# Values taken from a 384-column product and reordered over DRAM, in an attention phase on one core

## The reference

```python
hnorm = rms_norm(x, mixer_norm[layer])
qkv = (x @ w_in).reshape(b, s, 3, N_GROUPS, ATTN_HEADS, ATTN_HEAD_DIM)
for g, (window, dilation) in enumerate(((128, 1), (512, 4), (2048, 16))):
    q = rms_norm(qkv[:, :, 0, g], q_gain[g]) * (ATTN_HEAD_DIM ** -0.5)
    k = rms_norm(qkv[:, :, 1, g], k_gain[g])
    o, l = dilated_window_attention(q, k, qkv[:, :, 2, g], rel_bias[:, g], window, dilation)
wts = softmax(stack(lses), axis=0)
y = einsum('gbsh,gbshe->bshe', wts, stack(outs))
```

## Time and profile before

| | us |
|---|---|
| median of 3 runs (3330.32 to 3334.62) | 3331.82 |
| time of the profiled execution | 3333.34 |
| its span | 3331.6 |
| PE busy in it | 3162.4 (95%) |
| DVE, ACT, POOL busy | 1337.3, 1107.3, 824.0 |

### The profile page before, as it was taken

How to read it: one execution, slowest core, us unless ns; L and a number is a source line. 1 busy time by engine, 2 the same in 40 slices (tenths; PEclk the granted TensorE clock), 3 DMA queues, 4 the chain that set the end, 5 groups by cost and what they waited for, 6 DMA issues and landing times. The chain is left out here.

```text
span 3331.6 us, 48256 instructions
## 1 busy us (share of the span) xinstructions
PE 3162.4 (95%) x17466; PEld 2672.2 (80%) x17466; DVE 1337.3 (40%) x3725; ACT 1107.3 (33%) x3002; POOL 824.0 (25%) x598
## 2 busy tenths in 40 slices
PE   4999999999999995999999999899877999999999
PEld 3888888888888883878888888778665788888887
DVE  6446554555556554341313133531064431313131
ACT  4555555555555553321111112211254211111020
POOL 3333333333233310222222222222211222222221
PEclk9999999999999996999999999999898999999999
DMA  2112121221212114111111111111201111111112
GB/s 97 39 38 62 41 59 40 62 54 47 56 45 62 41 28 153 50 45 50 51 47 48 51 45 51 36 47 45 82 32 51 45 51 45 51 51 45 51 51 76
DMA packets 89904, 177.01 MB, mean 53 GB/s; under 512 B 25515, under 2 KB 55870, under 8 KB 89662
## 3 DMA queue, kind: packets, MB, share of 16 engines
q1 hardware_dynamic: 87358, 169.63, 16.4%
q10 hardware_dynamic: 2304, 4.20, 0.3%
HBM read 160.67 MB, written 13.12 MB: 52 GB/s over the span
## 5 line engine op out<-in xcount | busy, mean ns | idle before, releaser
L69 PE MATMUL ps_qk<-w_hi,attn_hT_hi 128*128 128x256 f32 x1536 | 439.1, 286 | 23.9 <-DVE attn_hT_lo L213 9.7
L915 POOL TENSOR_TENSOR first_w_lo<-first_raw,first_w_hi 128x1024 fp32r<-128x1024 f32 x96 | 231.5, 2411 | 886.0 <-ACT first_w_hi L911 886.0
L71 PE MATMUL ps_qk<-w_hi,attn_hT_lo 128*128 128x256 f32 x1536 | 437.6, 285 | 0.0
L70 PE MATMUL ps_qk<-w_lo,attn_hT_hi 128*128 128x256 f32 x1536 | 437.4, 285 | 0.0
L857 POOL TENSOR_TENSOR w_lo<-raw,w_hi 128x384 fp32r<-128x384 f32 x192 | 193.6, 1009 | 660.3 <-ACT w_hi L602 660.3
L915 POOL TENSOR_TENSOR second_w_lo<-second_raw,second_w_hi 128x1024 fp32r<-128x1024 f32 x72 | 172.3, 2393 | 620.6 <-ACT second_w_hi L911 620.6
L69 PEld LDWEIGHTS ps_qk<-w_hi,attn_hT_hi 128*128 128x128 f32 x1536 | 295.9, 193 | 28.2 <-issue 13.9
L70 PEld LDWEIGHTS ps_qk<-w_lo,attn_hT_hi 128*128 128x128 f32 x1536 | 296.6, 193 | 0.4
L71 PEld LDWEIGHTS ps_qk<-w_hi,attn_hT_lo 128*128 128x128 f32 x1536 | 296.4, 193 | 0.0
L69 PE MATMUL first_ps<-first_hid_hi,first_w_hi 128*128 128x512 f32 x640 | 250.9, 392 | 33.5 <-DVE first_hid_lo L1241 33.5
L635 ACT ACTIVATE prob<-ps_s,neg_max 128x128 f32<-128x128 f32 (+1 forms) x384 | 156.3, 412 | 362.4 <-DVE neg_max L726 362.4
(11 more groups left out here) (276 smaller groups left out, 6844.6 us busy)
## 6 DMA issues: line engine op xcount, KB each, us to landing
raw<-in_wqkv SPq DMA_DIRECT2D x192, 192.0 KB, 2.3
first_raw<-in_w SPq DMA_DIRECT2D x64, 512.0 KB, 3.4
second_raw<-in_w SPq DMA_DIRECT2D x64, 512.0 KB, 3.4
w_bc<-share_dram SPq DMA_DIRECT2D x48, 256.0 KB, 4.2
first_raw<-in_vo_pieces SPq DMA_DIRECT2D x16, 512.0 KB, 3.4
bias<-bias_dram SPq DMA_DIRECT2D x16, 256.0 KB, 3.4
yT_dram<-o_g SPq DMA_DIRECT2D x8, 512.0 KB, 3.1
first_raw<-in_attn_wo SPq DMA_DIRECT2D x8, 512.0 KB, 3.5
```

The source lines that it names most:

```text
L69: pe.matmul(out, a_hi, b_hi, start=first, stop=False)
L70: pe.matmul(out, a_hi, b_lo, start=False, stop=False)
L71: return pe.matmul(out, a_lo, b_hi, start=False, stop=last)
L915: pool.tensor_tensor(self.lo[:, n % 2, :], self.raw[:, n % self.RAW, :], self.hi[:, n % 2, :].bitcast(F32), ALU.subtract).then_inc(self.lo ...
```

## The change

What it does:

1. The value columns join the query and key columns: 24 products of 128x384 per step into `ps_qk` instead of 24 of 128x256 and 6 of 128x512. `ps_v`, `vT`, the transposes of `vT` and the two ACT copies per section are gone.
2. ACT copies the tile's values, 128x128, from `ps_qk` to `v_out` (a part of `ring`). SP writes them to `v_dram`, and after tiles 3 and 7 reads the half section back in the order of the group into `v_raw`.
3. ACT makes the high part of a unit's values out of `v_raw` (it was out of `ps_t`), and POOL the low part (DVE did it). On POOL it stands between the low part of the weights and `rs`.
4. PE's list is products, turned tiles, probabilities times values of the unit two back, turned probabilities of the unit one back, scores.
5. On ACT the turned tiles move from the end of the step to behind the exponentials, ahead of the outputs, the weights and the squares. On DVE they move from behind the sums of squares to behind the maxima.
6. The loop over supersteps is gone, all are written out.

```diff
-def run_supersteps(eng, step):
-    for st in range(LOOP_FIRST):
-        for j in range(TT):
-            step(0, st, j)
-    with eng.Fori(0, LOOP_COUNT) as i:
...
+def run_supersteps(step):
+    for st in range(LAST_SUPER + 1):
         for j in range(TT):
+            step(st, j)
...
+                if 1 <= T <= TT * SECTIONS:
+                    sec, t = divmod(T - 1, TT)
...
+                    sp.wait_ge(v_kept, T)
+                    sp.dma_start(v_dram[sec % 2, t * P:(t + 1) * P, :], v_out[:, t % 2, :]).then_inc(v_stored[t % 2], 16)
+                    if t % 4 == 3:
...
+                        for slot in range(2):
+                            sp.wait_ge(v_stored[slot], 16 * (T // 2))
+                        for dest, src in unit_order(sec, t // 4):
+                            sp.dma_start(dest, src).then_inc(v_in[t // 4], 16)
...
+                def products(ks):
...
+                    if T >= 2 and ks[0] == 0:
                         pe.wait_ge(qkn_done, T - 1)
-                    for k in range(KT):
+                        pe.wait_ge(v_kept, T - 1)
+                    for k in ks:
...
-                        mm = split_matmul(pe, ps_qk[j % 2][:, 0:2 * P],
+                        mm = split_matmul(pe, ps_qk[j % 2][:, 0:W3],
...
-                        mm = pe.transpose(ps_t[:, 2 * P:3 * P], vT[:, (st - 1) % 2, j * P:(j + 1) * P], ident[:])
...
-                    for k in range(2 * (j % 4), 2 * (j % 4) + 2):
-                        mm = split_matmul(pe, ps_v[:], w_hi[:, par, k, 2 * P:3 * P], w_lo[:, par, k, 2 * P:3 * P],
...
+                products(range(KT))
+                turn_tiles()
+                weigh_values()
+                turn_probabilities()
+                scores()
...
+                def unit_values():
+                    if has_unit(st, j, 1):
+                        sec, u = unit(st, j, 1)
+                        for half in halves_needed(sec, u):
+                            act.wait_ge(v_in[half], v_loads(sec))
+                        act.copy(v_hi[:, (U - 1) % 3, :], v_raw[:, sec % 2, u, :]).then_inc(v_hi_done, 1)
...
+                def squares_and_values():
...
+                        act.activation(sq[:], ps_qk[j % 2][:, 0:2 * P], ACT.Square).then_inc(squared, 1)
+                        if T >= 2:
+                            act.wait_ge(v_stored[j % 2], 16 * (T // 2))
+                        act.copy(v_out[:, j % 2, :], ps_qk[j % 2][:, 2 * P:W3]).then_inc(v_kept, 1)
...
+                exponentials()
+                turned_tiles()
+                outputs()
+                unit_values()
...
+                weights()
+                squares_and_values()
+                turned_probabilities()
...
+                        dve.wait_ge(rs_done, T + 1)
+                        dve.wait_ge(v_kept, T + 1)
...
+                maxima()
+                turned_tiles()
+                merge_step(st, j)
+                variances()
+                turned_probabilities()
+                normalise()
...
                     pool.wait_ge(w_hi_done, T + TT + 1)
                     lo_part(j % 4, (st + 1) % 2, j)
+                if has_unit(st, j, 1):
+                    sec, u = unit(st, j, 1)
+                    slot = (U - 1) % 3
+                    pool.wait_ge(v_hi_done, U)
+                    pool.tensor_tensor(v_lo[:, slot, :], v_raw[:, sec % 2, u, :], v_hi[:, slot, :].bitcast(F32),
+                                       ALU.subtract).then_inc(v_lo_done, 1)
                 if st < SECTIONS:
                     pool.wait_ge(var_done, T + 1)
```

More of the change, by code:

```diff
@@ L513, in step, with turn_tiles @@
                             pe.wait_ge(w_lo_done, TT * N + k + 1)
-                        mm = split_matmul(pe, ps_qk[j % 2][:, 0:2 * P],
+                        mm = split_matmul(pe, ps_qk[j % 2][:, 0:W3],
                                           hT_hi[:, k, j * P:(j + 1) * P], hT_lo[:, k, j * P:(j + 1) * P],
[L516 to L520, removed]
+                                          w_hi[:, par, k, :], w_lo[:, par, k, :], k == 0, k == KT - 1)
+                    if ks[-1] == KT - 1:
+                        mm.then_inc(qk_mm, 1)
+                def turn_tiles():
+                    rows = j == 1 and 2 <= st <= SECTIONS and (st - 2) % NG < 2
+                    tile = 1 <= T <= TT * SECTIONS
+                    if not (rows or tile):
+                        return
+                    if T >= 2:
                         pe.wait_ge(turn_hi, T - 1)
                         pe.wait_ge(turn_lo, T - 1)
-                    if TT * st + j - 1 < TT * SECTIONS:
+                    if tile:
                         pe.wait_ge(qkn_done, T)
@@ L535, in step, with weigh_values @@
                     mm.then_inc(turned, 1)
[L536 to L540, removed]
+                def weigh_values():
                     if has_unit(st, j, 2):
+                        sec, u = unit(st, j, 2)
+                        g = sec % NG
+                        whole = TT * sec + u
                         pe.wait_ge(p_hi_done, U - 1)
                         pe.wait_ge(p_lo_done, U - 1)
[L544 to L548, removed]
@@ L562, in step @@
[L562 to L568, removed]
+                        pe.wait_ge(v_hi_done, U - 1)
+                        pe.wait_ge(v_lo_done, U - 1)
+                        if has_unit(st, j, 3):
+                            pe.wait_ge(o_done, U - 2)
+                        first = 0 if has_prev(g, u) else 1
@@ L569, in step, with turn_probabilities @@
+                        for b in range(first, 2):
+                            slot = (whole - 1 + b) % 3
+                            mm = split_matmul(pe, ps_o[:, 0:2 * P], v_hi[:, slot, :], v_lo[:, slot, :],
+                                              pT_hi[:, b, :], pT_lo[:, b, :], b == first, b == 1)
+                        mm.then_inc(pv_done, 1)
+                def turn_probabilities():
                     if has_unit(st, j, 1):
+                        sec, u = unit(st, j, 1)
+                        g = sec % NG
@@ L579, in step @@
[L579 to L594, removed]
+                        if has_unit(st, j, 2):
+                            pe.wait_ge(p_hi_done, U - 1)
+                            pe.wait_ge(p_lo_done, U - 1)
@@ L626, in step @@
[L626 to L633, removed]
-                    for h in range(2):
-                        a = act.activation(prob[:, u % 2, h, c0:2 * P], ps_s[h][:, c0:2 * P], ACT.Exp,
-                                           bias=neg_max[:, sp_, h * TT + u:h * TT + u + 1],
-                                           accum_out=stat[:, sp_, (2 + h) * TT + u:(2 + h) * TT + u + 1])
-                    a.then_inc(exp_done, 1)
@@ new lines, in turned_tiles @@
+                def turned_tiles():
+                    if 1 <= T <= TT * SECTIONS:
+                        act.wait_ge(turned, T)
+                        sec, t = divmod(T - 1, TT)
+                        g = sec % NG
+                        for a in range(2):
+                            ins = act.activation(perm_dest(qk_hi[:, sec % 2, a, :], g, t * P, P),
+                                                 perm_view(ps_t[:, a * P:(a + 1) * P], g, P), ACT.Copy,
+                                                 scale=gains[:, a, g:g + 1])
+                        ins.then_inc(turn_hi, 1)
@@ new lines, in outputs @@
+                def outputs():
+                    if has_unit(st, j, 2):
+                        sec, u = unit(st, j, 2)
+                        g = sec % NG
+                        act.wait_ge(pv_done, U - 1)
+                        if u == 0:
+                            pair = sec // NG
+                            if g == 0 and pair >= 2:
+                                act.wait_ge(y_out, 16 * pair - 16)
+                            if g >= 1 and pair >= 1:
+                                act.wait_ge(y_step, 5 * pair - 5 + 2 * g)
+                        ob = o_raw[g][:, (sec // NG) % 2 if g == 0 else 0, :]
+                        act.copy(ob[0:HD, u * P:(u + 1) * P], ps_o[0:HD, 0:P])
+                        act.copy(ob[HD:P, u * P:(u + 1) * P], ps_o[HD:P, P:2 * P]).then_inc(o_done, 1)
```

356 lines of the change are left out of this document (178 added, 178 removed).

## The result

The changed kernel takes 3406.35 us (median of 4 runs, 3402.49 to 3409.79) against 3331.68 of the kernel before: ratio 1.0223, interval [1.0205, 1.0240]. It is slower, by 75 us. The forecast was 3407.

What follows compares the result with a forecast made beforehand. The prediction took a circle through DVE, ACT and POOL, avoiding PE, to bound the changed kernel. 73.6 - 1.7 - 0.3 + 13 - 10 = +75 on 3331.8 gave 3407 us, range 3355 to 3460.

Steps and rivals of the forecast that it cites:

- The direction and the bound: Whole kernel: 2.2% slower, with PE getting gaps and DVE, ACT and POOL setting the pace; slower 0.87.
- The circle's terms: Start-to-start times on DVE, ACT and POOL: 5.18 us before, 6.37 narrow and 6.85 wide after the change.
- the `qk_hi`: On ACT, the two come between exponentials and outputs and add 0.51 us per step.
- `v_hi`: On ACT, it comes ahead of `w_hi` and adds 0.20 us, at least 0.14, at most 0.28.
- the gap of 0.10: On POOL, 0.10 us between `w_lo` and `rs` where the two run back to back.
- the hand-over to DVE: From the end of POOL's `rs` to DVE: 0.05 us, estimated between nothing and 0.10.
- The merge: DVE's pieces delay the sums, 0.54 us too long each, two per pair; with small operations +13 us, between 0 and 25.
- PE's list: PE's work per step: 4.47 us removed, 4.20 or about 4.3 added; 0.21 us shorter, 5.97 on average.
- The loop: The hardware loop's two turns go when supersteps are written out: -10 us.
- The values over DRAM: Store and load between sections need at most 8.4 us of 11.5 us available, so they cost nothing.
- PE stays the bound: Rival: with a circle 0.63 us shorter than summed, PE's gain comes through, 3283 us; chance 10%.
- POOL and DVE disturb each other: Rival: POOL's `w_lo` and `v_lo` take 1.3 times as long, 0.45 us a step, +79, 3486 us; chance 8%.

Runs made afterwards that it cites:

- the first experiment: On POOL `v_lo` was put behind `rs` instead of ahead of it, against the changed kernel; 3367.99 us, ratio 1.0107.

## Why the prediction was right, point by point

**The direction and the bound: right, for the reason given.** The circle `qkn`, maxima, exponentials, `qk_hi`, outputs, `v_hi`, `w_hi`, `w_lo`, `v_lo`, `rs` sets the pace. Three edits that only change who stands behind whom on ACT, DVE and POOL take 107 us away. `v_lo` behind `rs` took 0.27 us from most steps, and the tiles late, away from j = 0, took 0.51 from wide ones (6.64 to 6.13), as such a circle must.

**The circle's terms: too long by 0.21 us.** "6.37 us" narrow was 6.16 (6.15 in the step shown), and 6.85 wide was 6.64. Of its terms `qkn` to exponentials (1.18 forecast, 1.19 measured), the `qk_hi` (0.51 and 0.50), `v_hi` (0.20 and 0.21), and `w_hi` to `w_lo` (0.59 and 0.59) were right. POOL's were too long: I took full durations, where `w_lo` to `v_lo` is 0.97 from start to start; `v_lo` is 0.41 to 0.42 and not 0.48; the gap of 0.10 ahead of `rs` is not there behind `v_lo`; and the hand-over to DVE is 0.03 after `rs` ends, 0.05 in the estimate. For the 176 steps this makes 83 x 6.64 + 93 x 6.16 = 1124 us instead of 1161: 37 us too many in the forecast.

**The merge: "+13, between 0 and 25" was too small.** Moving its pieces ahead of the turned tiles saves 32 us, outside that range. The step that failed is the pricing of a piece by the sums' delay alone: 0.54 for a piece of 2.03 us, where the piece shown cost 1.24, all of it in POOL's `w_lo`. I had kept the disturbance of POOL "inside their 25 us". The Trainium skill ("GPSIMD Engine Reference", section on the key structural facts) says that the two engines share their SBUF port. For DVE's sums beside `w_lo` the trace shows no cost to POOL, as I had said; for an operation of DVE with two operands in SBUF the trace agrees with a shared port: POOL all but stops.

**First steps of a superstep: left out.** 1139 us without the merge's cost are still 15 above 1124. In the run with the merge pieces first, the first step takes 6.87 us where the superstep's units are of group 1 or 2, 0.71 above a narrow one, and 6.58 for group 0, with 0.17 more two steps on; over 22 supersteps these make the 15 us. At j = 0 PE's scores wait for ACT's turned tiles (22 waits of the weight loads in the changed kernel, 18.2 us), and ACT then waits for PE's turned tiles in the step behind. The prediction's sum took all steps as alike, although the same steps of the kernel before are longer too.

Together: -37 for the circle, +19 for the merge, +15 for the first steps, which leaves the forecast 3 us above the measured window (1174 against 1171). Outside the window 2 us less were forecast and 4.7 less measured, the cause open. The profiled execution was then forecast 5.5 us too long (3408 against 3402.49), and it happens to be the shortest of the four. That the median of 3407 was hit is luck: these errors cancel.

**PE's list: right.** 0.17 us per product of 384 columns (0.175 forecast), and 0.22 us in a narrow step where PE bounds again, for 0.21. The forecast's own terms give 4.47 - 4.20 = 0.27 or, with "about 4.3", 0.17; 0.21 lies between them. The average step there is 6.05 us (1064.38 / 176) and not 5.97. **The loop: right**, 10 us by the windows and 8 by the medians, for 10. **The values over DRAM: right**, hidden with a step to spare; the two transfers take 5.4 us, where the forecast allowed 8.4.

**The rivals.** "PE stays the bound" would have needed a circle 0.63 us shorter; measured, it was 0.21 shorter. "POOL and DVE disturb each other" in every step did not occur, `w_lo`'s median being 1.015 us; it occurred beside the merge's pieces alone, and harder than the factor 1.30 (2.24 against 1.01).

## What to carry to other kernels

When an edit takes work off the bounding engine, follow the circles that avoid it: which instruction stands behind which on each other engine, and who hands over to whom. A helper of half a microsecond ahead of the one result that the circle carries made most steps 0.27 us longer here; behind that result it cost them nothing. Count a circle from start to start, and price the steps that differ (the first of a section, those with extra pieces) separately; one total that fits is no check of them.

## What the runs showed of the hardware

- A DVE operation on two float32 operands in SBUF (128x1024, 2.01 us) held POOL's subtraction up for nearly its whole length: 2.32 us instead of 0.46. DVE's reduction of one operand beside `w_lo` left it at 1.01 us. DVE's small `var` lasted 0.55 us where `w_lo` was held up, 0.22 in a narrow step, and ended 0.03 us after `w_lo`; why was not tried.
- POOL's `rs` (power) starts 0.10 us after the end of a 128x384 subtraction (and again in the first experiment), but 0.03 to 0.05 us before the end of a 128x128 one. Why was not tried.
- A turn of the hardware loop cost about 4 to 5 us with five engines in it: 8 us of median and 10 us of window for two.
